# Attention spread over the weight chunks beside it, and a head of half sets with spilled sums, in a two-layer decoder trunk

## What is computed

```python
def chunked_sgu(h, w_in, v_gain, w_s, b_s, w_out):
    u, v = jnp.split(jax.nn.gelu(h @ w_in), 2, axis=-1)
    v = rms_norm(v, v_gain).reshape(B, T // CHUNK, CHUNK, SGU_GROUPS, SGU_GROUP_DIM)
    sv = jnp.einsum('gts,bnsgc->bntgc', w_causal, v) + b_s.T[:, :, None]
    return (u * sv.reshape(B, T, SGU_WIDTH)) @ w_out
...
def nsa_attention(h, kv, w_in, q_gain, w_o):
    proj = h @ w_in
    q = rms_norm(proj[..., :N_HEADS * HEAD_DIM].reshape(B, T, N_KV, GROUP, HEAD_DIM), q_gain)
    gates = jax.nn.sigmoid(proj[..., N_HEADS * HEAD_DIM:])
    ...
        return g[:, :, 0] * o_cmp + g[:, :, 1] * o_slc + g[:, :, 2] * o_win
    return out @ w_o
```

## Time and profile before

| | |
|---|---|
| median of 3 runs | 2638.67 us (2631.64 to 2641.95) |
| the profiled execution | 2634.83 us, span 2633.1 us |
| busy: PE, VectorE, ScalarE, GpSimd | 2538.1, 2141.9, 1246.5, 379.2 us |
| mean granted clock of PE | 0.978 |
| moved by DMA | 685.49 MB, mean 260 GB/s |
| 3840 + 2176 matmuls of 512 columns | L1422, mean 399 and 397 ns |
| the chain that ended last | PE 86%, VectorE 7%, DMA 4%, ScalarE 2% |

### The profile page before, as it was taken

How to read it: one execution, slowest core, us unless ns; L and a number is a source line. 1 busy time by engine, 2 the same in 40 slices (tenths; PEclk the granted TensorE clock), 3 DMA queues, 4 the chain that set the end, 5 groups by cost and what they waited for, 6 DMA issues and landing times.

```text
span 2633.1 us, 38477 instructions
## 1 busy us (share of the span) xinstructions
PE 2538.1 (96%) x14006; PEld 2179.7 (83%) x14006; DVE 2141.9 (81%) x2569; ACT 1246.5 (47%) x1638; POOL 379.2 (14%) x205
## 2 busy tenths in 40 slices
PE   5789999998999999999998999899899999999999
PEld 4678888887888888888887888688788888888887
DVE  7967998899999888988898987678989756665666
ACT  2254443544554355435544444573455435543553
POOL 0000110131120011101142300273112001100110
PEclk8899999999999999999999989899999999999999
DMA  9978688886778877787766877207677655555544
GB/s 379 380 289 337 261 330 333 330 325 243 297 276 306 323 264 287 294 336 272 284 254 244 313 286 291 113 1 288 248 286 267 237 192 182 185 192 180 188 175 144
DMA packets 94311, 685.49 MB, mean 260 GB/s; under 512 B 10465, under 2 KB 10465, under 8 KB 11233
## 3 DMA queue, kind: packets, MB, share of 16 engines
q1 hardware_dynamic: 93746, 681.27, 68.7%
q10 hardware_dynamic: 432, 2.38, 0.2%
HBM read 681.51 MB, written 2.10 MB: 260 GB/s over the span
## 4 chain that ended last, share of the span: by engine, by line
PE 86%; DVE 7%; DMA 4%; ACT 2%; issue 1%; POOL 0%; SPq 0%; DVEq 0%; ACTq 0%
PE banks L1422 51%; PE banks L1424 26%; DMA raw<-in_stream 4%; DVE raw L1064 3%; DVE w_lo L1048 2%; PE banks L1391 2%; PE banks L1393 2%; PE banks L1394 2%; PE banks L761 1%; ACT w_hi L901 1%; DVE temp L1117 1%; PE banks L725 1%; PE banks L747 1%; PE banks L1411 1%; DVE scratch L831 1%
## 5 line engine op out<-in xcount | busy, mean ns | idle before, releaser
L1422 PE MATMUL banks<-h_op,w_hi 128*128 128x512 f32 x3840 | 1359.7, 399 | 22.7 <-DVE h_op L1123 18.7
L1048 DVE TENSOR_TENSOR w_lo<-raw,w_hi 128x1024 fp32r<-128x1024 f32 x841 | 1092.4, 1322 | 354.1 <-ACT w_hi L901 350.2
L901 ACT ACTIVATE w_hi<-raw 128x1024 fp32r<-128x1024 f32 x841 | 876.8, 1056 | 1023.9 <-PE banks L1424 616.3
L1424 PE MATMUL banks<-h_op,w_lo 128*128 128x256 f32 x3840 | 1078.4, 281 | 0.0
L1422 PEld LDWEIGHTS banks<-h_op,w_hi 128*128 128x128 f32 x3840 | 725.0, 189 | 203.9 <-issue 23.6
L1422 PE MATMUL banks<-act_op,w_hi 128*128 128x512 f32 x2176 | 765.5, 397 | 0.1
L1424 PEld LDWEIGHTS banks<-h_op,w_lo 128*128 128x128 f32 x3840 | 728.2, 190 | 0.0
L1424 PE MATMUL banks<-act_op,w_lo 128*128 128x256 f32 x2176 | 608.9, 280 | 0.0
L1064 DVE CUSTOM_DVE_ANT_0 raw<-raw,c_all 128x2048 f32<-128x2048 f32 x224 | 552.1, 2484 | 15.0 <-ACT c_all L875 9.7
L1422 PEld LDWEIGHTS banks<-act_op,w_hi 128*128 128x128 f32 x2176 | 409.4, 188 | 99.9 <-DVE w_lo L1048 0.9
L1424 PEld LDWEIGHTS banks<-act_op,w_lo 128*128 128x128 f32 x2176 | 411.2, 189 | 0.0
(11 more groups left out here) (156 smaller groups left out, 1361.6 us busy)
## 6 DMA issues: line engine op xcount, KB each, us to landing
raw<-in_stream SPq DMA_DIRECT2D x645, 1024.0 KB, 5.4
x_res<-in_x SPq DMA_DIRECT2D x1, 2048.0 KB, 11.4
out_x<-x_res SPq DMA_DIRECT2D x4, 512.0 KB, 5.0
mix_area<-in_w_s ACTq DMA_DIRECT2D x1, 1024.0 KB, 4.9
mix_area<-in_b_s ACTq DMA_DIRECT2D x1, 1024.0 KB, 8.2
small<-in_small SPq DMA_DIRECT2D x1, 682.0 KB, 16.2
attn_area<-in_pos ACTq DMA_DIRECT2D x1, 273.0 KB, 5.4
c_all<-in_c SPq DMA_DIRECT2D x1, 8.0 KB
```

What stands on the lines that cost most here:

```text
L901: act.activation(w_hi[:, out, 0:n], raw[:, slot, half:half + n], ACT.Copy).then_inc(hi_ready, 1)
L1048: dve.tensor_tensor(w_lo[:, out, 0:n], raw[:, slot, half:half + n], w_hi[:, out, 0:n].bitcast(F32), ALU.subtract).then_inc(stream, 2 if ch ...
L1422: pe.matmul(banks[:, g + j, :], hi[:, k, P * j:P * (j + 1)], operand[:, kt, :], start=(kt == 0), stop=False, skip_group_check=True)
L1424: last = pe.matmul(banks[:, g + j, 0:T], lo[:, k, P * j:P * (j + 1)], operand[:, kt, 0:T], start=False, stop=(kt == last_kt), skip_group_c ...
```

## The change

*Head.* sgu_v is gone. The head has eight half sets of four v chunks each, `HALF_SETS` = (half, quarter): (0,0), (1,0), (1,1), (0,1), (0,2), (1,2), (1,3), (0,3). The pattern has one mod piece behind each weight piece ("ssm"), h of a quarter is made at every second set. Eight banks hold four chunks, so a half's sums must leave: where the half changes, ScalarE copies them to SBUF (runs 0 and 1), or VectorE adds the banks to what is there (runs 2, 3, 4), and ScalarE applies Gelu to the finished sums (runs 3, 4) and squares them; all in between the sub-pieces of the next set. The mixing weights are loaded at the sixth set. Four mod pieces move to layer 0's up phases (`F3` for the first chunk, `P3` for the second of up00, `P3` for the second of up01 and up02).

*Order.* cmp (pattern F3, beside which the new h is made), gate, q (four chunks), wo.

*q.* Each tile takes three matmuls of 256 columns summed in one half bank (`one_sum`, also wo's first chunk): two banks for a chunk in place of four. ScalarE copies the sum (`q_copied`) and squares it; VectorE's addition falls away. Chunk 0 uses banks 2 and 3, chunks 1, 2, 3 and wo's first use 0 and 1.

*Attention.* By groups of four heads, in single steps placed by two tables behind sub-pieces of PE (`PE_ATTENTION`) and behind splits of ScalarE and VectorE (`SPLIT_ATTENTION`). Group g stands beside chunk g + 1 of q and the start of the next one, group 3 beside wo's first chunk. Queries are scaled before the scores. A head's two query blocks are one unit; VectorE's `tensor_tensor_reduce` adds the distance from a table (GpSimd builds the tables, 16 times 256 columns) and takes the minimum, out of PSUM; the exponential has scale -1. The compressed branch is done for four heads at once. vcmp is written four times, to 32-partition strips.

```diff
-N_POS = 2 * DW + 2
+N_POS = T + 2 * NCMP + 2
-    "H0": "mmmmmmmmE" + 4 * "ssmm",
-    "H": "E" + 4 * "ssmm",
-    "H3": "Essssssss",
+    "H0": "mmmmmmmmE" + 4 * "ssm",
+    "H": 4 * "ssm",
+    "HE": "E" + 4 * "ssm",
+HALF_SETS = [(0, 0, "H0"), (1, 0, "H"), (1, 1, "HE"), (0, 1, "H"), (0, 2, "HE"), (1, 2, "H"), (1, 3, "HE"),
+             (0, 3, "H")]
+RUN_ENDS = [0, 2, 4, 6, 7]
+RUN_STARTS = [0, 1, 3, 5, 7]
+for run, hs in enumerate(RUN_ENDS):
+    for i in range(4):
+        for table_, at in ((EVACUATE_V, 8 * hs + 2 * i + 4), (FINISH_V, 8 * hs + 2 * i + 5)):
...
-            phases.append(("q", [Chunk("q", 0, "F3", ("q", 0))]))
-            phases.append(("cmp", [Chunk("cmp", 0, "P0", ("cmp", 0))]))
-            phases.append(("q1", [Chunk("q", 1 + i, "P3", ("q", 0)) for i in range(3)]))
+            phases.append(("cmp", [Chunk("cmp", 0, "F3", ("cmp", 0))]))
             phases.append(("gate", [Chunk("gate", 0, "G1", ("gate", 0))]))
+            phases.append(("q", [Chunk("q", i, "P2" if i else "P3", ("q", 0)) for i in range(4)]))
             add("wo", ["dn"], 4, "P3", ("wo", 0))
...
+    for g in range(3):
+        for after, what, r in ((0, "sums", None), (2, "spread", None), (3, "score", 0), (4, "score", 1),
+                               (5, "turn_cmp", None), (6, "turn", 0), (6, "score", 2), (7, "weigh", 0),
+                               (7, "turn", 1), (7, "score", 3), (8, "weigh", 1), (9, "turn", 2), (10, "weigh", 2),
+                               (10, "turn", 3), (11, "weigh", 3)):
+            pe(g, after, what, r)
+        for after, what, r in ((3, "sums", None), (5, "spread", None), (6, "score", 0), (7, "score", 1),
+                               (7, "scale", 0), (8, "turn_cmp", None), (8, "scale", 1), (9, "turn", 0),
+                               (9, "score", 2), (10, "turn", 1), (10, "weigh", 0), (10, "score", 3), (10, "scale", 2),
+                               (11, "weigh", 1), (11, "scale", 3), (12, "turn", 2), (13, "weigh", 2),
+                               (13, "turn", 3), (14, "weigh", 3)):
+            split(g, after, what, r)
+    for after, what, r in ((0, "sums", None), (1, "spread", None), (2, "score", 0), (3, "score", 1),
+                           (4, "score", 2), (4, "turn_cmp", None), (5, "score", 3), (5, "turn", 0),
+                           (5, "weigh", 0), (5, "turn", 1), (5, "weigh", 1), (6, "turn", 2), (6, "weigh", 2),
+                           (6, "turn", 3), (6, "weigh", 3)):
+        pe(3, after, what, r)
...
         def free_wait(eng, cur):
             if cur.first.kind == "vh":
                 return
+            if PHASE_OF[id(cur.first)] == "sgu_u0" and cur.first.loc < 2:
+                eng.wait_ge(v_added, 10 + 2 * cur.first.loc)
+                return
+            if cur.first.kind == "q" and cur.first.loc >= 2 or cur.first.source == ("wo", 0) and cur.first.loc == 0:
+                eng.wait_ge(q_copied, cur.first.loc if cur.first.kind == "q" else 4)
+                return
...
+                if e == 0 and kind == "q":
+                    done_wait(act, prev)
...
+                    act.activation(q, banks[:, q_bank(prev.first):q_bank(prev.first) + 2, :].rearrange("p a t -> p (a t)"),
+                                   ACT.Copy).then_inc(q_copied, 1)
+                    act.wait_ge(q_copied, k + 1)
+                    act.activation(q_squares(k), q, ACT.Square).then_inc(queries_squared, 1)
...
+            if what == "score":
+                dve.wait_ge(tables_built, g + 1)
+                dve.wait_ge(qk_done, n + 1)
...
+                    last = dve.tensor_tensor_reduce(
+                        part, banks[:, 4 + qb, keys * b:keys * (b + 1)], table(g, r)[:, T - keys:T], -1.0, 3e38,
+                        ALU.add, ALU.min, stat(n, NEG, k, 1))
...
+                if r == 0:
+                    dve.wait_ge(cmp_zeroed, 1)
+                    for j in range(GRP):
...
+            def add_v(run, hs, i):
...
+                for n in range(2):
+                    part = v_tiles(4 * half + i, n)
+                    last = dve.tensor_tensor(part, v_bank(i, n), part, ALU.add)
+                last.then_inc(v_added, 1)
...
                 if name == "wo":
-                    pe.wait_ge(out_lo, 4 * (u + 1))
+                    pe.wait_ge(out_lo, 2 * (u + 1))
...
+                            if run and cur.first.hs == RUN_STARTS[run] and u % 2 == 0:
+                                if run <= 2:
+                                    pe.wait_ge(v_copied, 4 * (run - 1) + u // 2 + 1)
+                                else:
+                                    pe.wait_ge(v_added, 4 * (run - 3) + u // 2 + 1)
```

More of the change, by code:

```diff
@@ L125, in is_looped @@
 def is_looped(name, chunks):
-    return len(chunks) >= 6 and name != "kv"
+    return len(chunks) >= 6 and name not in ("kv", "head")
 def plan():
@@ L136, in add @@
                               for i in range(count)]))
-    phases.append(("head", [Chunk("vh", i, p, ("sgu_v", 0)) for i, p in enumerate(("H0", "H", "H", "H3"))]))
-    phases.append(("sgu_v", [Chunk("v", 4 + i, "P3", ("sgu_v", 0)) for i in range(4)]))
+    phases.append(("head", [Chunk("vh", quarter, p, ("sgu_v", 0)) for _, quarter, p in HALF_SETS]))
+    for hs, ch in enumerate(phases[0][1]):
+        ch.hs, ch.half = hs, HALF_SETS[hs][0]
     for half in range(2):
@@ new lines, in place_attention, with pe, split @@
+def place_attention():
+    def pe(g, after, what, r=None):
+        c, u = divmod(after, 8)
+        key = ("q", g + 1 + c, u) if g + 1 + c < 4 else ("wo", g - 3 + c, u)
+        PE_ATTENTION.setdefault(key, []).append((what, g, r))
+    def split(g, after, what, r=None):
+        c, u = divmod(after, 8)
+        key = ("q", g + 1 + c, u) if g + 1 + c < 4 else ("wo", g - 3 + c, u)
+        SPLIT_ATTENTION.setdefault(key, []).append((what, g, r))
+    for g in range(3):
[15 more added lines that the diff above has]
+        pe(3, after, what, r)
+    for after, what, r in ((3, "sums", None), (4, "spread", None), (5, "score", 0), (6, "score", 1),
+                           (6, "scale", 0), (7, "score", 2), (7, "turn_cmp", None), (7, "scale", 1),
+                           (8, "score", 3), (8, "scale", 2), (8, "turn", 0), (8, "weigh", 0), (8, "turn", 1),
+                           (8, "weigh", 1), (9, "scale", 3), (9, "turn", 2), (9, "weigh", 2), (10, "turn", 3),
+                           (10, "weigh", 3)):
+        split(3, after, what, r)
@@ L228 @@
+place_attention()
 class At:
@@ new lines, in prologue_act @@
+        def prologue_act(act, what):
+            if what == "keys":
+                act.wait_ge(cmp_done, 1)
+                for r in range(GRP):
+                    last = act.activation(vcmp[32 * r:32 * r + NCMP, :], banks[32 * r:32 * r + NCMP, 6, :], ACT.Copy)
+                act.activation(sq_c, banks[:, 5, 0:NB], ACT.Square).then_inc(cmp_keys_squared, 1)
+                act.wait_ge(square_sums, 1)
+                act.activation(r_k, banks[0:16, 7, 0:T], ACT.Sqrt, scale=1.0 / HD, bias=eps[0:16, :])                     .then_inc(rms_taken, 1)
+            if what == "cmp_keys":
+                act.wait_ge(square_sums, 2)
+                act.activation(r_c, banks[:, 5, 0:NB], ACT.Sqrt, scale=1.0 / HD, bias=eps[:, :]).then_inc(rms_taken, 1)
+            if what == "spread_keys":
+                act.wait_ge(zsum, BY_NAME["gate"][0].n["zsum"] + 1)
+                act.activation(gates_t, gates_t, ACT.Sigmoid).then_inc(gates_ready, 1)
@@ new lines, in attention_pool @@
+        def attention_pool(pool):
+            pool.wait_ge(h_ready, KT * (h_index("cmp") + 1))
+            pool.memset(spare[:, 1536:1792], 0.0).then_inc(cmp_zeroed, 1)
+            pool.wait_ge(pos_loaded, 32)
+            pool.wait_ge(cmp_done, 1)
+            build_table(pool, 0)
+            build_table(pool, 1)
+            for g in range(NKV):
+                for r in range(GRP):
+                    n = GRP * g + r
+                    pool.wait_ge(coef_ready, n + 1)
+                    for k, (qb, b, part) in enumerate(parts(n)):
+                        last = pool.tensor_scalar(part, part, stat(n, COF, k, 1), None, ALU.mult)
+                    last.then_inc(weights_scaled, 1)
+                if g < 2:
+                    build_table(pool, g + 2)
@@ L1140, in evacuate @@
                     mix_tiles(dve, group(cur))
[L1141 removed]
+                if e == 0 and kind in ("ua", "uv", "u", "kvf", "cmp", "gate"):
                     dve.wait_ge(zlo, prev.val(lambda c: c.n["zlo"] + 1))
@@ L1178, in evacuate @@
                         kt = TPC * prev.first.loc + j
+                        if one_sum(prev.first):
+                            half = slice(P * part, P * (part + 1))
+                            dve.scalar_tensor_tensor(
+                                out=x[:, kt, half], in0=banks[:, j // 2, T * (j % 2) + P * part:T * (j % 2) + P * (part + 1)],
```

(3 more changed lines are left out.)

747 lines of the change are left out of this document (433 added, 314 removed).

## The result

The changed kernel takes 2679.15 us (median of 4 runs, 2678.24 to 2680.4), the kernel before 2635.52 beside it: ratio 1.0157, 95% interval 1.0142 to 1.0173. It is slower by some 43 us (41 by the ratio, which goes by all runs and not by medians); the forecast was 2633, in a range of 2600 to 2665. The profiled execution has a span of 2678.6 us, 45.5 more than before's.

What follows compares the result with a forecast made beforehand. PE is busy 96% of 2633.1 us, so only its waits or lower rate can yield. Head -26, moved mod pieces +1, attention stage +20 give -5 on 2634.83, 2629.8; the median is 3.8 above: 2633, range 2600 to 2665.

Steps and rivals of the forecast that it cites:

- the head's -26: Head: sgu_v's weight pieces move in, last v weight done at 224 in place of 252.93; -26 us (-12 to -34).
- the 1 us for the clock behind the new waits: Attention stage: PE beginning again at the lower clock after waits, counted as 1 us (0 to 8).
- dense part: Attention stage: 8 chunks of 64 pairs at 0.346, 177 us; three 256-column matmuls add 0 (to +2).
- Scalar's copies (8 of two halves) lie in its idle half: Head: ScalarE's copies of sums add no time; PE (216), DMA (217) and VectorE (207) are the three bounds.
- the hole around the mixing stays: After the head: the hole in PE's work around the mixing is unchanged by the edit.
- rival C: Head: weight, weight, mod order starves PE, 6 us a pair for 5.47, ends near 238, gain 12; 2647, chance 0.10.
- Order around the compressed keys: Before q: cmp runs while h is made, gate waits for its weight; q starts 38.7 us after kv's end.
- Attention's work: Attention in PE's queue: 4.5 us a head, 5.8 a group, prologue 13; sum 108 us.
- Waits: Attention stage: added waits of 12.6 (q2, q3, wo0), 6 (transposes), 12 (wo0), prologue 2; 33.6 with clock (10 to 50).
- the rule beside it: Trainium skill: groups of matmuls with waits between each start cold; at three boundary waits, stage 6 us longer.
- A (waits absorbed): Attention stage: waits mostly absorbed, only boundaries (9 of 12.6) left, stage -4, total -29; 2609, chance 0.32.
- B (GpSimd slows VectorE's splits): Attention stage: GpSimd's scaling beside VectorE's splits delays the chain, 5 us on five chunks, +25; 2658, chance 0.20.

Runs made afterwards that it cites:

- e2: Kernel before with the change's head alone, old attention, and ScalarE's Gelu moved behind its next split: 2621.59 us, 0.9926 to before.
- e3: Changed kernel with ScalarE's Gelu of a finished sum moved behind its next split: 2665.77 us, 1.0108 to before.
- e6: Changed kernel with useless matmuls on TensorE ahead of its longest waits, which stay: 2663.36 us, 1.0088 to before.
- e4: Changed kernel with ScalarE's copy of q out of PSUM one split earlier, in three q chunks and wo's first: 2667.75 us, 1.0112 to before.
- e7: Changed kernel with the spread of the queries' norms cut in two halves, a sub-piece of dense work between: 2683.91 us, 1.0173 to before.
- e5: Changed kernel with VectorE scaling a head's weights in place of GpSimd: 2676.93 us, 1.0124 to before.
- e8: Changed kernel with the edits of e3, e4, e5 and e7 together: 2654.17 us, 1.0050 to before.
- e9: Changed kernel with e3, e4 and e6's useless matmuls, none at the chunks' starts: 2641.98 us, 1.0002 to before.

## Why the prediction was wrong

The steps that failed are two terms of the sum: the head's -26, for which ScalarE's queue was never walked (measured -6.8), and the 1 us for the clock behind the new waits (measured 27.8). The dense part was a little low, and the rest came out nearly as worked out.

*Head, failed.* Forecast: last v weight at 224 (216 to 238), -26 held to the end. Measured: 239, and -6.8 at the second chunk of sgu_u0 (-3 to -8 in the six profiles with this head). The step that failed is "Scalar's copies (8 of two halves) lie in its idle half": I took three engines as three separate bounds and never walked ScalarE's queue. With the Gelu moved, the last v product is at 228.7 (e2), inside the range. A second part failed too: "the hole around the mixing stays". From the first product of sgu_u0 to its second chunk it was 37.6 us and is 44.0 now. PE waits there 2.3 us for low parts and 2.75 for the mixing's operands, before not at all; that the last run's additions and Gelus, which moved into it, cause these waits is argued, not tested. Its test of wrongness, PE waiting for splits all through the head, didn't come: this is not rival C's cause, though its size (a gain of 12) was nearer.

*Order around the compressed keys, right.* q starts 39.1 us after the last product of kv began; forecast 38.7.

*Attention's work, nearly right.* A head is 4.5 us and a group 5.8 by starts in the trace, as worked out; the prologue 9.6 for 13.

*Dense part, low.* "Three 256-column matmuls in place of 512 + 256 stream the same 768 columns, cost 0 (to +2 ...)": they follow each other at 0.12, a pair is 0.36 for 0.346, 4.5 us on five chunks. wo's other chunks at the slower pitch, 192 pairs at 0.3533 for 0.346: 1.4.

*Waits, right in kind and size.* Forecast 32.6 without the clock, measured 29.2: 10.5 at q2, q3 and wo0 (12.6), released by ScalarE's copy as said; 8.5 ahead of the turned weights (6); 10.2 in wo's first chunk (12), of which the first was to be 4.18; prologue 0 (2). Only the one ahead of the transposes was put down to the wrong chain: GpSimd's scaling releases it, not the compressed weights.

*Clock, the larger error.* "I count 1 for it (0 to 8)". It cost 27.8 us in the changed kernel's profile (24.7 in e3's, whose stage is the same). The prediction had the row that shows it, behind the earlier trace rows, and set aside the rule beside it as worth 6 us at most, counted for three boundaries only. What it missed is that half rate strikes attention's matmuls as well as dense ones, that it comes behind the waits ahead of the transposes too and three times without a wait, and that in wo's first chunk, with waits of 0.8 to 4.2 us one after the other, the clock stays down for 17 and 10 us. The first of these waits matters most: with it filled (e6) both stretches are gone, the second perhaps by chance. Against before only 15.8 of the 27.8 are new, since before's attention had lost 12.0 in the same way; the forecast got its +20 from before's stage with that loss inside, but priced its own without.

Sum for the stage: 357.3 + 0.4 + 4.5 + 1.4 - 3.4 (prologue) - 3.4 (waits) + 26.8 (clock) = 383.6; measured 385.9 (1529.18 to 1915.07). 2.3 us are not placed. The forecast's -5 against 45.5 in the profiles is then the stage 28.6, the head 19.2, the pitch 4.8 and -2 of small ones.

*Rivals.* A (waits absorbed) is out: e4 shows the first three on the path in full. B (GpSimd slows VectorE's splits) came nearest in time, 2658, with a mechanism that did not happen: low parts are 1.22 us. C's cause is out, above. No rival had the clock as its mechanism, and that is what the range lacked.

## What to carry to other kernels

When work is spread between dense matmuls, price each new wait of TensorE twice, its own length and the half-rate work behind it, and look for waits that follow each other. Where two engines split a stream, walk each queue through one period of the steady state, with every operation placed between the splits: a bound per engine hides a ring. Where a wait can't be removed, useless matmuls in it may pay: 6 to 16 us in three kernels here.

## What was not expected of the hardware

- Useless work on TensorE made a kernel faster, 15.8 us in the changed one and 7.4 in the one before.
- The same instructions at full granted clock run at one of two pitches, 0.3467 or 0.3533 us a pair, that changes between phases and between executions of one program. What sets it is open; it moves the 345 us of the sgu phases by 5 us.
- Runs of narrow matmuls (4 partitions in, or 120 columns, as in cmp of the kernel before, window below) go with half rate although PE doesn't wait in them. Only e7 touches this, so it is seen, not shown.
- A wait of one and the same length is followed by half rate in one execution and not in another (2.47 us in wo's first chunk: not in e3 and e6, but in the changed kernel, e4, e5, e7, e8 and e9).

```profile
1564.00:1584.00 20.00, 20.00 (x96) 20.00 (x96) 8.93 (x8) 6.27 (x6) 0.00 (x0) 0.50 0.67 263
```
